# A two-layer encoder step: residual held transposed, norms without transposes, and a second feed-forward product with stationary weights, mostly by seven products

## The reference

```python
def _rms(x, g):
    xf = x.astype(jnp.float32)
    y = xf * lax.rsqrt(jnp.mean(xf * xf, axis=-1, keepdims=True) + EPS) * g.astype(jnp.float32)
    return y.astype(x.dtype)
...
    h = _rms(x, p['norm_mix'])
...
    x = x + (ga * ya + gb * yb + gc * yc) @ p['w_o']

    h2 = _rms(x, p['norm_ffn'])
    gt, up = jnp.split(h2 @ p['w_ffn_in'], 2, axis=-1)
    x = x + (jax.nn.silu(gt) * up) @ p['w_ffn_out']
```

## Time and profile before

| | |
|---|---|
| runs | 2117.05, 2118.14, 2118.57 us |
| span of the profiled execution | 2115.1 us, some 3 us below the median of the runs; the rest lies outside the span |
| TensorE, matmul | 2088.8 us, 99% |
| VectorE | 1393.8 us, 66% |
| ScalarE | 964.3 us, 46% |
| GpSimd | 395.3 us, 19% |
| chain that ended last | TensorE 90%, VectorE 4%, ScalarE 3% |
| DMA | 98 GB/s on average |

### The profile page before, as it was taken

The page is one execution under the profiler, slowest core; times in us unless marked ns, Lnnn a source line. Parts: engine busy times, 40 slices in busy tenths (PEclk is TensorE's granted clock), DMA queues, the critical chain, the costliest instruction groups (busy, mean ns, idle before and its releaser), DMA issues.

```text
span 2115.1 us, 36960 instructions
## 1 busy us (share of the span) xinstructions
PE 2088.8 (99%) x13616; PEld 1878.8 (89%) x13616; DVE 1393.8 (66%) x2839; ACT 964.3 (46%) x2054; POOL 395.3 (19%) x287
## 2 busy tenths in 40 slices
PE   9999999999999999999999999999999999999999
PEld 8998878888979989989899987788899899899897
DVE  4467876646749838739445778766476696496493
ACT  4336676566335314324232467665663353243241
POOL 1120030300014214224011200203000152241230
PEclk9999999999999999999999999999999999999999
DMA  6234234132322222222232332241413212122222
GB/s 221 76 111 126 71 102 137 61 136 91 131 79 88 83 80 90 81 80 80 79 139 77 111 116 89 81 139 63 172 64 133 93 68 90 70 90 81 80 90 80
DMA packets 90682, 207.84 MB, mean 98 GB/s; under 512 B 20676, under 2 KB 46920, under 8 KB 90184
## 3 DMA queue, kind: packets, MB, share of 16 engines
q1 hardware_dynamic: 90504, 205.48, 28.8%
HBM read 181.50 MB, written 23.95 MB: 97 GB/s over the span
## 4 chain that ended last, share of the span: by engine, by line
PE 90%; DVE 4%; ACT 3%; issue 1%; DVEq 1%; POOL 1%; DMA 0%; SPq 0%; ACTq 0%
PE ps L902 28%; PE ps L948 15%; PE ps L1433 8%; PE ps L1435 8%; PE ps L1434 8%; PE ps L960 7%; PE ps L1124 2%; PE ps L1144 2%; PE ps L1020 2%; PE ps L1065 1%; PE ps L1238 1%; PE ps L1039 1%; PE ps L1413 1%; PE ps L1203 1%; POOL rsq L1974 1%
## 5 line engine op out<-in xcount | busy, mean ns | idle before, releaser
L1494 ACT ACTIVATE w_hi<-raw 128x1024 fp32r<-128x1024 f32 (+4 forms) x172 | 171.2, 998 | 399.5 <-PE ps L902 369.3
L2029 DVE TENSOR_TENSOR w_lo<-raw,w_hi 128x1024 fp32r<-128x1024 f32 (+4 forms) x124 | 139.1, 1123 | 180.1 <-ACT w_hi L1494 176.1
L948 PE MATMUL ps<-h_hi,w_hi 128*128 128x320 f32 x768 | 246.1, 320 | 0.0
L948 PE MATMUL ps<-h_hi,w_lo 128*128 128x320 f32 x768 | 237.2, 309 | 0.0
L948 PE MATMUL ps<-h_lo,w_hi 128*128 128x320 f32 x768 | 237.2, 309 | 0.0
L1433 PE MATMUL ps<-th_hi,op_hi 128*128 128x320 f32 x640 | 197.8, 309 | 4.0 <-issue 4.0
L1974 POOL TENSOR_TENSOR rsq<-ssq,mhalf 128x12 f32<-128x12 f32 (+3 forms) x56 | 117.1, 2092 | 443.1 <-DVE ssq L2107 383.2
L1435 PE MATMUL ps<-th_hi,op_lo 128*128 128x320 f32 x640 | 197.9, 309 | 0.0
L1434 PE MATMUL ps<-th_lo,op_hi 128*128 128x320 f32 x640 | 197.7, 309 | 0.0
L902 PE MATMUL ps<-w_hi,act_hi 128*128 128x512 f32 x440 | 174.5, 396 | 0.0
L902 PE MATMUL ps<-w_lo,act_hi 128*128 128x512 f32 x440 | 174.4, 396 | 0.0
(11 more groups left out here) (376 smaller groups left out, 5401.7 us busy)
## 6 DMA issues: line engine op xcount, KB each, us to landing
raw<-in_weights SPq DMA_DIRECT2D x212, 512.0 KB, 3.3
gates<-gst SPq DMA_DIRECT2D x72, 160.0 KB, 1.8
g<-gates SPq DMA_DIRECT2D x12, 960.0 KB, 6.3
raw<-in_weights SPq DMA_DIRECT2D x24, 384.0 KB, 2.9
ktb<-in_cache_fox_kt SPq DMA_DIRECT2D x16, 384.0 KB, 4.2
vc<-in_cache_fox_v SPq DMA_DIRECT2D x16, 384.0 KB, 3.7
x_sb<-in_x_prompt SPq DMA_DIRECT2D x8, 512.0 KB, 5.1
out_y_prompt<-x_sb SPq DMA_DIRECT2D x8, 512.0 KB, 3.4
```

What stands on the lines that cost most here:

```text
L948: mm = pe.matmul(ps[:, 5, 0:HALF], w[:, kk * P:(kk + 1) * P], h_pair[x][:, kk, half * HALF:(half + 1) * HALF], start=kk == 0 and n == 0, s ...
L1494: return act.activation(dst, src, ACT.Copy, scale=scale)
L2029: dve.tensor_tensor(low[:, 0:width], raw[raw_slot(c)][:, 0:width], high[:, 0:width].bitcast(F32), ALU.subtract).then_inc(lo_made.sem, 1)
```

## The change

The residual, the input and the output are held transposed: 8 tiles of 128 features by 640 tokens. The host passes the input and takes the output in that form. The tokens are handled in two parts, of 256 and 384.

A norm squares each tile (ScalarE), adds the squares up (GpSimd, in the opening partly VectorE), sums over the partitions by small products with ones (`norm_sum`), takes the root, writes the roots on diagonals (VectorE), spreads them over all partitions by a product with ones (`norm_spread`), and VectorE scales each tile by spread and gain. No transposes are left in it.

The output projection and the last four feed-forward steps use the weights as stationary operand and stream 256 or 384 tokens (`block_part`). The other 18 steps of the second product are done in 12 units of seven products: six steps of 128 by two output tiles by two halves of the tokens. Two neighbouring steps make a pair, whose activations `ff_act` are combined by four differences and split into seven operands `a_hi`, `a_lo`. The units stand after step 6, 12 and 18 in one common sequence with the seven-product steps of the first product. Chunks of an output unit are 768 wide instead of 1024.

```diff
--- before.py
+++ after.py
@@ -54,53 +54,98 @@
 
 
 GROUPS = [(1158, 384), (1542, 296), (0, 384), (384, 384), (768, 390), (1838, 416)]
-FF_GROUPS = [8, 8, 6]
+FF_GROUPS = [6, 6, 6, 4]
+FF_STEPS = sum(FF_GROUPS)
+FF_AT = [sum(FF_GROUPS[:_q]) for _q in range(len(FF_GROUPS))]
...
+UNITS = []
+for _j in range(FF_STEPS):
+    UNITS.append(("in", _j))
+    if _j in FF_AT[1:]:
+        UNITS += [("out", 4 * (FF_AT.index(_j) - 1) + _n) for _n in range(KD // 2)]
+FAST = UNITS[FF_PLAIN:]
+LAST = len(FAST) - 1
+C_ROWS = C_FF + 2 * len(UNITS)
...
+
+            return 4 * ((FF_PLAIN + s + 1) % 2) + (0, 1, 2, 3, 0, 2, 3)[i]
...
+                def norm_sum(q, p, L=L):
+
...
+                    for n, t in enumerate(PART_TILES[p]):
+                        for k, rows in enumerate((square_sum[:, t * P:(t + 1) * P], squares[:, 1, t * P:(t + 1) * P])):
+                            mm = pe.matmul(ps[:, norm_banks(q, L, p)[0], 2 * n:2 * n + 2], rows, cst("ones", 0, 2), start=k == 0, stop=k == 1)
+                    mm.then_inc(ln_summed.sem, 1)
+
+                def norm_spread(q, p, L=L):
+
+                    pe.wait_ge(diag_made.sem, diag_made.at(L, 2 * q + p + 1))
+                    tiles = diag[:, PART_TILES[p].start:PART_TILES[p].stop, :].rearrange("p t n -> p (t n)")
+                    pe.matmul(ps[:, norm_banks(q, L, p)[1], 0:part_width(p)], cst("ones"), tiles, start=True, stop=True).then_inc(ln_spread.sem, 1)
...
+                def block_part(c, x_pair, k0, j, p, first, last, bank):
+
+                    for kk in range(2):
+                        for n, (w, x) in enumerate(w_of(c)):
+                            mm = pe.matmul(ps[:, bank, 0:part_width(p)], w[:, 512 * kk + j * P:512 * kk + (j + 1) * P], x_pair[x][:, k0 + kk, PARTS[p]],
+                                           start=first and kk == 0 and n == 0, stop=last and kk == 1 and n == 2)
+                    return mm
...
+                def block_last(c, x_pair, k0, first, banks, bank_free, between):
+
+                    pe.wait_ge(lo_made.sem, lo_made.at(L, MADE[c]))
+                    for j in range(4):
+                        if first:
+                            bank_free(2 * j)
+                        block_part(c, x_pair, k0, j, 0, first, False, banks[2 * j])
+                    pe.wait_ge(lo_made.sem, lo_made.at(L, MADE[c + 1]))
+                    for j in range(4):
+                        block_part(c + 1, x_pair, k0 + 2, j, 0, False, True, banks[2 * j]).then_inc(cols_done.sem, 1)
+                    for j in range(4):
+                        if first:
+                            bank_free(2 * j + 1)
+                        mm = block_part(c, x_pair, k0, j, 1, first, False, banks[2 * j + 1])
+                        if j == 3:
+                            mm.then_inc(w_used.sem, 1)
+                        if j == 2:
+                            between(1)
+                        block_part(c + 1, x_pair, k0 + 2, j, 1, False, True, banks[2 * j + 1]).then_inc((w_used if j == 3 else cols_done).sem, 1)
+                        if j == 0:
+                            between(0)
 
                 h_pair, mix_pair, act_pair = (h_hi, h_lo), (mix_hi, mix_lo), (act_hi, act_lo)
...
-                def product(c, i, bank, first):
-
-                    pe.wait_ge(lo_made.sem, lo_made.at(L, BASE[c] + i + 1))
-                    for kk in range(4):
-                        x_hi, x_lo = OPERAND_H[i](kk)
+                def product(s, i):
+
+                    pe.wait_ge(lo_made.sem, lo_made.at(L, made_by(s, i)))
+                    bank, first, tiles = product_bank(s, i), i < 4, fast_width(s) // P
+                    for kk in range(tiles):
+                        x_hi, x_lo = OPERAND_H[i](kk) if FAST[s][0] == "in" else (a_hi[i][:, kk, :], a_lo[i][:, kk, :])
                         a = slice(kk * P, kk * P + P)
                         pe.matmul(ps[:, bank, 0:HALF], op_hi[i][:, a], x_hi, start=first and kk == 0, stop=False, skip_group_check=not first)
                         pe.matmul(ps[:, bank, 0:HALF], op_hi[i][:, a], x_lo, start=False, stop=False, skip_group_check=not first)
-                        mm = pe.matmul(ps[:, bank, 0:HALF], op_lo[i][:, a], x_hi, start=False, stop=kk == 3, skip_group_check=not first)
+                        mm = pe.matmul(ps[:, bank, 0:HALF], op_lo[i][:, a], x_hi, start=False, stop=kk == tiles - 1, skip_group_check=not first)
...
+                def sum_squares(q, layer, items):
+
+                    for k, p in items:
+                        a = square_sum[:, PARTS[p]]
+                        pool.wait_ge(squared.sem, squared.at(layer, 2 * KD * q + square_at(q + layer == 0, k, p) + 1))
                         pool.drain()
-                        pool.tensor_tensor(lnr[:, t:t + 1], lnss[:, t:t + 1], mhalf[:, 0:1], ALU.pow).then_inc(ln_root.sem, 1)
...
+                def scaled(q, p, k, layer=L):
+
+                    if k == 0:
+                        dve.wait_ge(ln_spread.sem, ln_spread.at(layer, 2 * q + p + 1))
+                    spread = ps[:, norm_banks(q, layer, p)[1], 0:part_width(p)]
+                    dve.scalar_tensor_tensor(hx[q][:, k, PARTS[p]], x_sb[:, k, PARTS[p]], norm_gain[:, 2 * layer + q, k:k + 1], spread,
+                                             ALU.mult, ALU.mult).then_inc(ln_x.sem, 1)
...
+                def pair_total(m, r):
+
+                    dst, a, b = ((pair_first(m), ff_act[0][:, second], ff_act[0][:, first]), (ff_act[0][:, second], ff_act[1][:, second], ff_act[0][:, second]),
+                                 (ff_act[0][:, first], ff_act[1][:, second], pair_first(m)), (ff_act[1][:, first], ff_act[1][:, first], ff_act[0][:, first]))[r]
                     dve.drain()
...
+                    dve.tensor_tensor(dst, a, b, ALU.subtract).then_inc(pair_sum.sem, 1)
...
+                def pair_low(m, r):
+
+                    i, src = ((0, ff_act[0][:, first]), (4, ff_act[1][:, first]), (6, ff_act[1][:, second]), None,
+                              (2, ff_act[0][:, second]), (1, ff_act[0][:, first]))[r]
+                    dve.wait_ge(pair_hi.sem, pair_hi.at(L, 7 * m + r + 1))
+                    dve.tensor_tensor(a_lo[i][:, m % 3, :], src, a_hi[i][:, m % 3, :].bitcast(F32), ALU.subtract).then_inc(pair_lo.sem, 1)
...
+                            dve.wait_ge(first_out.sem, first_out.at(L, s + 1))
+                            summed(part[0][:, :], sg[:, s % 2, second], 1)
+                            dve.drain()
+                            if kind == "out":
+                                three = x_sb[:, n, second]
+                                three = bass.AP(tensor=three.tensor, offset=three.offset, ap=[list(three.ap[0]), [HALF, 3], [1, HALF]])
+                                dve.tensor_tensor(three, three, rows_bcast(part[0][:, :], 3), ALU.add)
+                                dve.drain()
+                        if i == 2 and kind == "in":
+                            summed(part[1][:, :], part[0][:, :], 2)
+                            dve.drain()
+                        if i == 3 and kind == "in":
+                            summed(part[1][:, :], part[1][:, :], 3)
+                        if i in (2, 3) and kind == "out":
+                            summed(beside_it[:, second], beside_it[:, second], i)
+                            dve.drain()
+                        if i == 4 and kind == "out":
+                            dve.wait_ge(w_used.sem, w_used.at(L, used_by(s, 4)))
+                            dve.tensor_tensor(column[:, first], column[:, first], at(4), ALU.add)
...
+                            dve.drain()
+                            mul(ff_act[j % 2][:, first], sg[:, s % 2, first], part[2][:, :])
+                        if i == 5 and kind == "out":
...
+                        if i == 6 and kind == "in":
+                            summed(part[0][:, :], part[0][:, :], 6)
+                        if i == 6 and kind == "out":
+                            summed(column[:, second], column[:, second], 6)
...
+OUTPUTS = [("y_t", (KD, P, NTOK))] + [
```

1352 lines of the change are left out of this document (714 added, 638 removed), and 2 rows, old and new, of the table HOME.

## The result

The changed kernel takes 2190.14 us (median of 4 runs, 2189.56 to 2190.50) against 2117.60 (4 runs, 2116.93 to 2118.57): ratio 1.0341, 95% interval 1.0329 to 1.0354. It is 72.5 us slower; the forecast was 2098, 20 faster, and the range ended at 2113.

The account below looks back on a forecast made before the run. The prediction took TensorE's sum of matmul pitches to bound the kernel. Its terms, -31 + 2 - 13 + 6 - 6 + 2 + 5 + 15 = -20, took the 2115.1 us span to 2095, or 2098 us with 3.0 outside; range 2079 to 2113.

Parts of the forecast that it names:

- Fast steps, +15: Seven-product steps with pairs and output units: VectorE runs late, 2.5 us per group, six groups, adding 15 us.
- the rival "slower": Pairs of first-product steps: VectorE and GpSimd exclude one another, 27.8 us against 24.64, 2141 us in all; chance 0.09.
- The sign named for the rival: In the fast steps, steps of 13 us or more at every pair would show that VectorE and GpSimd exclude one another.
- The count of 11.9 of 12.32: Seven-product step before the change: 6.5 us of two-input VectorE work plus 5.4 of GpSimd fill 11.9 of 12.32 us.
- the rival's 58: Extra time if VectorE and GpSimd exclude one another: 3.2 us per pair of first-product steps, 58 us in all.
- Waits inside a layer, -6: Output projection to second feed-forward step and early products: norm waits, about 4.3 us a layer, mostly hidden; saves 6 us.
- transposes, -13: The three norms other than the opening one: 15 groups of eight transposes at 0.88 us disappear, saving 13 us.
- +6 for three norms: Ten small products with ones and two spreads per norm replace the transposes, about 2.0 us each, adding 6 us.
- Opening, +5: First norm and projection: 120 projection matmuls through at 45 to 47 us against 40.35, adding 5; bounds 0 and +12.
- Between the layers, +2: Norm chain between the layers, with an extra weight split in front: 3 us of waits against about 1, adding 2.
- Second product, -31: Second feed-forward product: 18 chunks a layer become 12 seven-product units, 126.4 to 110.9 us, saving 31 for both layers.

Follow-up runs that it names:

- e1: Changed kernel, GpSimd's four weight sums narrowed to 8 columns from the third seven-product unit of a layer on; 2118.17 us, ratio 1.0002.
- e13: Kernel before the change, a fifth 512-wide GpSimd operation added in each seven-product step from the third of a layer on; 2141.57 us, ratio 1.0111.
- e9: Changed kernel, the 960-wide addition of each output unit narrowed to 12 columns; 2183.50 us, ratio 1.0308.
- e12: Changed kernel, GpSimd's four weight sums at half their width from the third unit on; 2124.81 us, ratio 1.0034.
- e7: As e3, with GpSimd's work at the start of the seven-product steps moved to VectorE too; 2153.38 us, ratio 1.0168.
- e11: As e7, with VectorE's weight sums narrowed to 8 columns from the third unit on; 2109.82 us, ratio 0.9962.
- e3: Changed kernel, each unit's four weight sums and GpSimd's two remainders per pair moved to VectorE; 2161.26 us, ratio 1.0204.
- e6: Changed kernel, 8 and 10 more unread products in the opening where TensorE waits; 2190.16 us, ratio 1.0343.
- e5: Changed kernel plus a final measuring stretch of VectorE operations and GpSimd sums, alone and together; eight sums take 9.97 us alone, 13.41 beside two-SBUF operations.

## Why the prediction was wrong

**Fast steps, +15: this step failed.** It measured 72 (e1). My text had the mechanism and the price: the rival "slower" worked a pair out at 27.8 us, and the trace has 28.14. The sign named for the rival, steps of 13 us or more at every pair, is there: 15.5 and 15.4. What I did with it was wrong in four places.
- "Against it: today's step with the same kind of load costs TensorE nothing." A stage at TensorE's pace says that VectorE isn't late, not that it has room. e13 shows that a run of steps had none: one more sum makes each of them 1.08 us longer. The count of 11.9 of 12.32 had said so.
- For the pair I added the new operations at their undisturbed 0.42 to 0.5 and 0.9 of stretch for GpSimd's remainders. But new two-SBUF operations also meet sums that they did not meet before. The nine of a pair bring 4.1 us undisturbed; the row at 819.51 alone shows 3.07 for two of them. Net per pair: 3.1 (15.5 against 12.4 in e1), where I had 0.7 to 1.9 less a slack.
- At the group's first output unit I counted 0.7 to 1 us for the last remainder of the last pair. TensorE waits 3.2 to 3.3 us there, six times, 19.5 us, since the remainder stands behind stretched operations, and then runs its next dozen matmuls at the lower clock.
- The output unit should have given 0.2 back each. It gives nothing: 9.4, 9.3, 10.1, 11.3 against 9.24, and 8.7, 9.2, 9.4, 9.7 in e1. These are 2.6 of the 11.7 us of a group, 16 in all, and that is why the rival's 58 was short of 72 too; its place and price were right. The 960-wide addition, 1.38 instead of 1.2, is only a part of it (e9: 6.6 us when it is all but taken away); the rest is argued, not shown: the four sums of such a unit come in turn with its seven splits.

The queue depth that was to "swallow" part of it does so in e12, where the unit behind a pair's 14.0 takes 10.6; in the changed kernel it takes 12.6.

**Waits inside a layer, -6, and transposes, -13.** The stretch from the output projection on was to shrink by 5 us a layer and grew by 4.8. The transposes are gone, but the term for the products in their place, +6 for three norms, was read at half its size. The trace has two entries for one plain f32 product: the "twenty" of the earlier trace rows are ten products of the program, and two of a norm's four first ones read

```profile
631.88 0.28 PE L986 MATMUL ps<-consts,square_sum 128*128 128x2 f32 x2
632.02 0.36 PE L986 MATMUL ps<-consts,squares 128*128 128x2 f32 x2
```

Each such product costs 0.22 us, not 0.115, and the spreads of 256 and 384 columns 0.42 and 0.64 instead of 0.23 and 0.35. From start to start the products of one norm take 3.4 us where 2.0 were counted: +10 instead of +6. More of the miss is elsewhere: I followed the norm's chain only to its last scaled tile and not into what stands behind it on VectorE: the 1280-wide differences and remainders, up to 4.29 instead of 1.49 us, since GpSimd has 1280-wide ones and the first weight sums at the same time. TensorE waits 6.29 us for the first operand. With GpSimd cleared the stretch is 0.7 to 1.5 us shorter than before (e7 and e11, both layers), so the same mechanism took some 6 of the 9.8 us. Of the other 4 the products are 1.4. The spread and scaling chain was not longer than I counted: up to the first seven-product matmul TensorE waits 1.3 us in layer 0 of e7 (0.17, 0.77 and 0.40), where 1.5 were forecast. The last 2 to 3 us stay open.

**Opening, +5.** Measured 13.2, with the 120th matmul at 53.44 instead of 45 to 47. The first spread came at 20.34 instead of 17.8, and the pair of tiles for which the first projection matmul waits was split at 24.74 instead of 21.3: 2.5 us late before the spread and 0.9 behind it, where VectorE has four additions of the second part instead of three ahead of the splits. And from 26.0 to 36.3 the granted clock was 0.51, so that the 384-wide matmuls have a pitch of 0.32. The second spread stands behind them and came at 37.30, though its diagonal was ready at about 34. The clock was missing from the forecast. The five traces that have less of the lower level there (e1, e3, e6, e11, e12) have an opening 3.3 to 4.5 us shorter, and what becomes of that in the whole time stays open.

**Between the layers, +2.** In e1, where VectorE keeps up, feed-forward 1 is 13.2 us shorter than before and feed-forward 0 with the next norm only 9.0. The norm behind it thus costs 4.2 where my terms (transposes -4.4, products +2, waits +2) gave 0.4 back: a miss of 4 to 5 us. The products at their true price are 1.4 of it; no run shows the rest.

**Second product, -31.** Right where VectorE keeps up: the group of e1 in the table above takes 111.1 against 110.9 counted.

The Trainium skill (SBUF — State Buffer, section on the two separate sides) says that the shared port pair goes to whichever operation starts first, for its whole length, and that only VectorE operations with two SBUF inputs (or in a fast mode) are concerned. By that rule, e5 agrees in both halves: 13.41 against 9.97 us for eight sums in turn, 10.03 beside the operations that read PSUM.

## What to carry over

When two engines take turns on something, add up their turns as if they were one engine, and compare the sum with the pitch of the bound; a stage that runs at the bound's pace tells nothing of the reserve, and a cheap run with one more operation per step does. Work moved into such a stage is priced by the operations that it will meet, not by its undisturbed time. If a change puts two fillings of one engine back to back (pair, then output units), count each unit's list on its own, and the start of the stage as a unit too.
